# Seven block products for half of the down projection's columns, with the weight differences on GpSimd

## The reference

```python
def swiglu(x, w_gate, w_up, w_down):
    return (jax.nn.silu(x @ w_gate) * (x @ w_up)) @ w_down

h = h + swiglu(rms_norm(h, norm2_g[i]), ffn_w_gate[i], ffn_w_up[i], ffn_w_down[i])
```

## Time and profile before

| what | value |
|---|---|
| median of three runs | 1424.87 us |
| profiled execution, first to last instruction (span) | 1422.4 us |
| TensorE busy | 1395.2 us, 98% |
| VectorE busy | 944.7 us, 66% |
| ScalarE busy | 691.0 us, 49% |
| GpSimd busy | 82.9 us, 6% |
| moved by DMA | 239.47 MB, 168 GB/s on average |
| one ring slot of 1.5 MB, issue to landing (median) | 6.6 us |

### The profile page before, as it was taken

The page is one execution under the profiler, slowest core; times in us unless marked ns, Lnnn a source line. Parts: engine busy times, 40 slices in busy tenths (PEclk is TensorE's granted clock), DMA queues, the critical chain, the costliest instruction groups (busy, mean ns, idle before and its releaser), DMA issues. The chain is left out here.

```text
span 1422.4 us, 25483 instructions
## 1 busy us (share of the span) xinstructions
PE 1395.2 (98%) x10044; PEld 1286.2 (90%) x10044; DVE 944.7 (66%) x1539; ACT 691.0 (49%) x1107; POOL 82.9 (6%) x137
## 2 busy tenths in 40 slices
PE   8999999999999999999999999999999999999997
PEld 8898888999989999899989999999998988899997
DVE  5778567766668666567577666676665676676665
ACT  6764545433454443376654433444433655643342
POOL 1030010000020000000000000100000123000000
PEclk9999999999999999999999999999999999999999
DMA  9344005645526555433356545365554423465540
GB/s 359 135 160 185 2 25 228 222 177 183 197 108 228 209 184 177 178 104 133 120 207 224 189 177 182 129 229 198 194 177 178 149 90 134 177 222 180 194 158 30
DMA packets 33069, 239.47 MB, mean 168 GB/s; under 512 B 6864, under 2 KB 13280, under 8 KB 14304
## 3 DMA queue, kind: packets, MB, share of 16 engines
q1 hardware_dynamic: 30320, 234.84, 45.6%
q10 hardware_dynamic: 2672, 3.58, 0.7%
HBM read 236.15 MB, written 2.25 MB: 168 GB/s over the span
## 5 line engine op out<-in xcount | busy, mean ns | idle before, releaser
L498 PE MATMUL ps<-uT_h,w_gu 128*128 128x256 f32 x3520 | 614.1, 279 | 2.5 <-ACT uT_h L1316 2.5
L498 PEld LDWEIGHTS ps<-uT_h,w_gu 128*128 128x128 f32 x3520 | 538.0, 188 | 13.8 <-issue 5.0
L498 PE MATMUL ps<-uT_l,w_gu 128*128 128x256 f32 x1760 | 478.8, 279 | 0.0
L498 PE MATMUL ps<-w_dn,h_r 128*128 128x512 f32 x1320 | 325.7, 396 | 0.3 <-DVE h_r L2070 0.3
L498 PEld LDWEIGHTS ps<-uT_l,w_gu 128*128 128x128 f32 x1760 | 325.5, 188 | 0.0
L498 PEld LDWEIGHTS ps<-w_dn,h_r 128*128 128x128 f32 x1320 | 239.6, 188 | 51.3 <-issue 1.4
L1368 ACT CAST w_gu<-ring 128x2048 fp32r<-128x2048 f32 x110 | 210.0, 1909 | 156.2 <-PE ps L498 155.6
L2028 DVE TENSOR_TENSOR w_gu<-ring,w_gu 128x2048 fp32r<-128x2048 f32 x110 | 252.1, 2292 | 35.2 <-ACT w_gu L1368 35.2
L2061 DVE TENSOR_TENSOR us<-ps,bc 128x256 f32<-128x256 f32 x110 | 46.5, 423 | 203.2 <-PE ps L498 203.2
L1381 ACT ACTIVATE wk<-wk 128x256 f32<-128x256 f32 x110 | 46.1, 419 | 260.7 <-DVE wk L2059 260.7
L1374 ACT CAST w_dn<-ring 128x1024 fp32r<-128x1024 f32 x110 | 115.7, 1052 | 82.8 <-PE ps L498 82.7
(11 more groups left out here) (398 smaller groups left out, 1696.0 us busy)
## 6 DMA issues: line engine op xcount, KB each, us to landing
ring<-wstream SPq DMA_DIRECT2D x144, 1536.0 KB, 6.6
cst<-consts_in SPq DMA_DIRECT2D x1, 2185.0 KB, 13.7
wk<-t_row ACTq DMA_DIRECT2D x1, 2048.0 KB, 8.0
wk<-masks_in SPq DMA_DIRECT2D x1, 1216.0 KB, 24.1
x<-x_in SPq DMA_DIRECT2D x2, 512.0 KB, 4.7
ring<-wstream SPq DMA_DIRECT2D x1, 1024.0 KB, 8.8
inh<-gains ACTq DMA_DIRECT2D x2, 512.0 KB, 9.6
tri_blocks<-wk SPq DMA_DIRECT2D x3, 256.0 KB, 2.8
```

Source lines behind the costliest of these rows:

```text
L498: return pe.matmul(o, l, r, start=start, stop=stop, skip_group_check=True)
```

## The change

Chunks 0 to 17 are taken in 9 pairs (PAIRS). The columns of the down weights are reordered into four blocks of 256. For two of them, a pair is a product of 2 x 2 blocks: two token tiles by two chunks for h, two chunks by two column blocks for the weights. It is made of seven block products instead of eight, in the form of Strassen and Winograd: four sums of h blocks (forms, on VectorE), four differences of weight blocks (x_diff and y_diffs, on GpSimd), and seven products that are summed over the pairs in seven half banks of PSUM. After the ninth pair VectorE puts them together and adds them to the residual stream (combine). The other two column blocks, and all columns of chunks 18 to 21, are computed as before.

The sums over the pairs need PSUM, so gate and up have one bank each (4 and 6; chunk 1 alone uses 5 and 7). The down part of a chunk comes two steps after its gate and up instead of one: the X products (two of seven, with the even chunk's plain half) after up of an even step, the Y products (five, with the odd chunk's plain half) after up of the next. The factor bc is left out of up and put on the sum of the down products at the end (row_scale). The split of all eight h blocks is one copy on ScalarE and one subtraction on VectorE for each pair. The down weights move in the stream: slot c holds those of chunk c-2, and each feed-forward has one slot more, 23. Six steps are written out before the loop, which has three rounds. Elsewhere some semaphores are merged into one with steps.

```diff
-        LOOPS = (FC - 6) // 4
+        LOOPS = (PLAIN - LOOP_FROM) // 4
+        IN_X = [(0, 0, 7, 256), (2, 768, 5, 0)]
+        IN_Y = [(3, 1024, 0, 0), (5, 1792, 0, 256), (4, 2048, 2, 0), (6, 2304, 5, 256), (7, 2560, 7, 0)]
+        def gu_bank(c, m):
+            return ps[(5, 7)[m] if c == 1 else (4, 6)[m]][:, 0:T]
...
+            def products(p, these):
+                for i, ws, bank, lo in these:
+                    for n, (a, b) in enumerate(PASSES):
+                        last = mm(ps[bank][:, lo:lo + 256], h_r[a][:, i * P:(i + 1) * P], w_d[b][:, ws:ws + 256],
+                                  p == 0 and n == 0 and i in STARTS_BANK, p == PAIRS - 1 and n == 2)
+                return last
...
                 def step(c, r=0):
-                    pe.wait_ge(s["lo_a"], r + (q + c + 1))
-                    if q + c >= 2:
-                        pe.wait_ge(s["h_ready"], r + (q + c - 1))
+                    n, pairs = q + c, 2 * (PAIRS * f + c // 2 - 1)
+                    def up_free():
+                        if c == 1:
+                            spread_rstd(norm)
+                        else:
+                            pe.wait_ge(s["h_mul"], r + (n - (c == 2)))
+                    pe.wait_ge(s["lo_a"], r + (n + 1))
                     if c == 0:
...
                         first_gate_up(norm)
                     else:
-                        gate_up(c, (lambda: spread_rstd(norm)) if c == 1 else None)
-                    if 0 < c < FC - 1:
-                        pe.wait_ge(s["lo_b"], r + (q + c))
-                        pe.wait_ge(s["h_ready"], r + (q + c))
...
-                        down(c - 1, c == 1)
+                        if c > 1:
+                            pe.wait_ge(s["gs_ready"], r + (n - (c == 2)))
+                        gate_up(c, up_free)
...
+                    if 2 <= c < PLAIN + 2:
+                        if c % 2 == 0:
+                            pe.wait_ge(s["bx_ready"], r + (pairs + 2))
+                            pe.wait_ge(s["form_lo"], r + (pairs + 2))
+                            products(c // 2 - 1, IN_X)
+                            for t in range(TT):
+                                last = down_part(c - 2, t, 1)
+                            last.then_inc(s["dx_done"], 2)
+                        else:
+                            pe.wait_ge(s["by_ready"], r + (pairs + 2))
+                            for t in range(TT):
+                                down_part(c - 2, t, 1)
+                            products(c // 2 - 1, IN_Y).then_inc(s["dy_done"], 2)
+                    if PLAIN < c < FC:
+                        if c < FC - 1:
+                            down(f, c - 1)
...
+            def x_blocks(f, p, r=0):
+                i, n = BASE[f"ffn{f}"] + 2 * p + 2, 2 * (PAIRS * f + p)
+                if n:
+                    act.wait_ge(s["dx_done"], r + n)
+                act.copy(w_d[0][:, 0:768], slot(i)[:, 2 * D:2 * D + 768]).then_inc(s["bx_hi"], 1)
+                act.wait_ge(s["bx_diff"], r + (n + 2))
+                act.copy(w_d[0][:, 768:1024], diffs[:, 768:1024]).then_inc(s["bx_hi"], 1)
+            def y_blocks(f, p, r=0):
...
+                act.copy(w_d[0][:, 1024:2048], slot(i)[:, 2 * D:3 * D]).then_inc(s["by_hi"], 1)
+                act.wait_ge(s["by_diff"], r * 2 + (2 * n + 4))
+                act.copy(w_d[0][:, 2048:2816], diffs[:, 2048:2816]).then_inc(s["by_hi"], 1)
+            def forms_hi(f, p, r=0):
...
+                act.wait_ge(s["form_ready"], r * 2 + (2 * n + 4))
+                act.copy(h_r[0][:, :], misc[:, 0:8 * P]).then_inc(s["form_hi"], 2)
...
                     act.activation(sg[:, c % 2, :], sg[:, c % 2, :], ACT.Silu).then_inc(s["silu_ready"], 1)
                     if c + 2 < FC:
                         hi_a(f, c + 2, r, rr)
...
+                    if c < PLAIN:
+                        if c % 2:
+                            forms_hi(f, p, r)
+                        else:
+                            x_blocks(f, p, r)
+                    else:
+                        if c < PLAIN + 2:
+                            hi_b(f, c)
+                        if c == PLAIN + 1:
+                            act.copy(xn[:, 0, 0:512], ps[7][:, :]).then_inc(s["p_copied"], 1)
+                        act.wait_ge(s["h_mul"], n + 1)
+                        hs = c % 2 * 3 * P
+                        act.copy(h_r[0][:, hs:hs + T], sg[:, c % 2, :]).then_inc(s["h_hi"], 1)
...
+            def x_diff(f, p, r=0):
...
+                gp.wait_ge(s["hi_a"], r + (FC * f + 2 * p + 3))
...
+                gp.tensor_tensor(diffs[:, 768:1024], b12, b11, ALU.subtract).then_inc(s["bx_diff"], 2)
+            def y_diffs(f, p, r=0):
...
+                gp.wait_ge(s["hi_a"], r + (FC * f + 2 * p + 4))
...
+                gp.tensor_tensor(t3, b22, b12, ALU.subtract).then_inc(s["by_diff"], 1)
...
+                gp.tensor_tensor(t2, t3, b11, ALU.add).then_inc(s["by_diff"], 1)
...
+                gp.tensor_tensor(t4, b21, t2, ALU.subtract).then_inc(s["by_diff"], 2)
...
                 def step(c, r=0):
...
                     v.wait_ge(s["gu_gate"], r + (n + 1))
-                    v.tensor_tensor(h, ps[4 + c % 2][:, 0:T], bc[:], ALU.mult).then_inc(s["gs_ready"], 1)
+                    v.tensor_tensor(h, gu_bank(c, 0), bc[:], ALU.mult).then_inc(s["gs_ready"], 1)
+                    if c % 2 == 0 and 2 <= c <= PLAIN:
+                        y_lo(f, p - 1, r)
+                    if c % 2 and c < PLAIN:
+                        x_lo(f, p, r)
                     v.wait_ge(s["gu_ps"], r + (n + 1))
-                    v.tensor_tensor(us[:], ps[6 + c % 2][:, 0:T], bc[:], ALU.mult).then_inc(s["us_ready"], 1)
...
+                    v.tensor_tensor(to, two(h), two(up), ALU.mult).then_inc(s["h_mul"], 1)
+                    if c % 2 and c < PLAIN:
+                        forms(f, p, r)
                     if c + 2 < FC:
                         lo_a(f, c + 2, r)
...
+                    elif c % 2:
+                        forms_lo(f, p, r)
+                    if c == PLAIN + 1:
+                        combine(f)
```

More of the change, by code:

```diff
@@ L23 @@
 RING = 4
+PAIRS = 9
+PLAIN = 2 * PAIRS
+LOOP_FROM = 6
 NC_CMP, CMP_STRIDE = 15, 16
@@ L153, in build @@
         w_gu = over("w_gu", [P, 2, 2, 2 * D], "wk")
-        w_dn = over("w_dn", [P, 2, 2, D], "wk", 8 * D)
-        h_r = over("h_r", [P, 2, 2, T], "ffb")
+        w_d = [over(f"w_d{i}", [P, 2816], "wk", 8 * D + i * 2816) for i in range(2)]
+        h_r = [over("h_r0", [P, 8 * P], "ffb"), over("h_r1", [P, 8 * P], "inh", 2 * D)]
         ring_r = over("ring_r", [P, RING, SLOT], "ring")
@@ L549, in _, with gate_up @@
             PASSES = [(0, 0), (1, 0), (0, 1)]
-            def gate_up(j, between=None):
+            def gate_up(j, between):
                 for m in range(2):
-                    if m and between:
+                    if m:
                         between()
@@ new lines, in y_lo @@
+            def y_lo(f, p, r=0):
+                i, n = BASE[f"ffn{f}"] + 2 * p + 2, 2 * (PAIRS * f + p)
+                v.wait_ge(s["by_hi"], r + (n + 1))
+                v.tensor_tensor(w_d[1][:, 1024:2048], slot(i + 1)[:, 2 * D:3 * D], w_d[0][:, 1024:2048].bitcast(F32),
+                                ALU.subtract)
+                v.wait_ge(s["by_hi"], r + (n + 2))
+                v.tensor_tensor(w_d[1][:, 2048:2816], diffs[:, 2048:2816], w_d[0][:, 2048:2816].bitcast(F32),
+                                ALU.subtract).then_inc(s["by_ready"], 2)
+                v.wait_ge(s["by_ready"], r + (n + 2))
+                for k in range(2):
+                    v.sem_inc(s[f"free{(i + k) % RING}"], 1)
@@ new lines, in forms_lo, with lo_b @@
+            def forms_lo(f, p, r=0):
+                n = 2 * (PAIRS * f + p)
+                v.wait_ge(s["form_hi"], r + (n + 2))
+                v.tensor_tensor(h_r[1][:, :], misc[:, 0:8 * P], h_r[0][:, :].bitcast(F32), ALU.subtract
+                                ).then_inc(s["form_lo"], 2)
+            def lo_b(f, c):
+                i, lo = BASE[f"ffn{f}"] + min(c + 2, FC), 2 * D if c + 2 < FC else (c + 2 - FC) * D
+                e, ws = 4 * f + c - PLAIN, c % 2 * D
+                v.wait_ge(s["hi_b"], e + 1)
+                v.tensor_tensor(w_d[1][:, ws:ws + D], slot(i)[:, lo:lo + D], w_d[0][:, ws:ws + D].bitcast(F32),
@@ L2642, in _ @@
               "g23_ready")
-            ffn(0, 1.0)
+            ffn(0, 1.0, rstd(1))
             norm(3)
-            ffn(1, 0.5)
+            ffn(1, 0.5, small[:, 6:8])
             norm(4)
```

344 lines of the change are left out of this document (226 added, 118 removed).

## The result

The changed kernel took **1437.68 us** (median of 4 runs, 1436.37 to 1438.62) where the kernel before, on the same chip, took 1424.99 (1424.51 to 1425.17): a ratio of 1.0089, with a 95% interval of 1.0074 to 1.0103. It is 0.9% slower. The forecast was 1435.5, with 1424 to 1448 around it. The profiled execution spans 1435.9 us, 13.5 more than before; the mean granted clock is 0.994, where it was 0.999.

What follows compares the result with a forecast made beforehand. TensorE, busy 98% of the span, was taken to bound the kernel. -15.75 + 13.6 + 9.25 + 1.45 + 2.1 = +10.65 us on the 1422.4 span, plus 2.5 for launch and end, gave 1435.5 us; range 1424 to 1448.

Steps and rivals of the forecast that it cites:

- gate(2) behind lo_a(2): Step 2 of each feed-forward: TensorE pauses 2.8 us for lo_a(2), 2.4 in feed-forward 0; 13.6 us in all.
- first X products behind form_lo: Pair 0 of each feed-forward: TensorE waits 1.85 us for forms_lo; 9.25 us in five, bounds 6.75 and 17.7.
- gate(3) of feed-forward 1: Feed-forward 1: gate(3) waits for gs(2), which stands behind first_block in VectorE's queue; 1.45 us.
- tails: Ends of feed-forwards 0, 2 and 3: TensorE waits for chunk 21's h, 0.9, 0.9 and about 0.3; 2.1 us.
- The starts: Steps 0 and 1 lose their down part, so TensorE waits twice per start: at gate(2), 13.6 us, and pair 0, 9.25.
- the addition for GpSimd: First pair: 0.5 us, taken once per start, for y_diffs slipping between VectorE's operations; raises the pause from 1.35 to 1.85.
- the prediction's sentence on the rule: First pair: GpSimd and VectorE operations exclude each other; one subtraction let in whole before forms_lo would add 1.2 us.
- The prediction's 2.43 us row: Profile of the kernel before: a GpSimd operation released beside lo_a(1) lasted 2.43 us, ending with it; cited for the exclusion rule.
- The saving: Down products of 9 pairs in 5 feed-forwards: 2.80 us become 2.45 each, 15.75 us less TensorE work.
- The rival of the clock: Clock falls to 1.2 GHz in the starts' pauses, so step 2 runs slower: 1453 to 1467 us; chance 0.05.
- The other steps costed at nothing: Steady pairs without waits, combine's eight additions in step 19, and the 23rd slot's DMA: each costs nothing.
- The faster rival: The starts' pauses do not open, leaving 15.75 less the 2.1 at the end: 1411 us; chance 0.13.

Runs made afterwards that it cites:

- experiment 1: Changed kernel with ScalarE's hi_a(2) ahead of the copy of bc and VectorE's lo_a(2) ahead of the first gate's scaling; 1422.51 us, ratio 0.9988.
- experiment 7: Changed kernel with hi_a(2), lo_a(2) early, first_block spread over steps 2 to 5, last h copy early, and forms_lo(0) ahead of lo_a(3); 1414.81 us, ratio 0.9932.
- experiment 8: Changed kernel with 20 unused 256-column matmuls ahead of the wait for lo_a(2) in each feed-forward; 1437.17 us, ratio 1.0087.
- experiment 2: Changed kernel with feed-forward 1's four first_block operations placed one behind each of steps 2 to 5; 1435.04 us, ratio 1.0074.
- experiment 3: Changed kernel with ScalarE's copy of h for chunk 21 ahead of hi_a of the next feed-forward; 1434.94 us, ratio 1.007.
- experiment 4: Changed kernel without GpSimd's weight differences, ScalarE and VectorE reading the plain weight blocks in the same sizes; 1433.92 us, ratio 1.0061.
- experiment 6: Changed kernel with an eighth product, three more 256-column matmuls, in each pair; 1452.45 us, ratio 1.0194.

## Why the prediction was right

By its own steps, the forecast beside what the profiled execution shows:

| Step | Forecast, us | Measured, us | Shown by |
|---|---|---|---|
| TensorE work taken away, 45 pairs | -15.75 | -13.95 | pair of 16.49 against 16.80 |
| gate(2) behind lo_a(2), five | +13.6 | +12.4 (waits: 13.3) | starts of gate(2), below; experiment 1 |
| first X products behind form_lo, five | +9.25 | +8.4 | 7.24 to 7.33 from gate(2), less 5.6; experiments 7, 8 |
| gate(3) of feed-forward 1 | +1.45 | +2.2 (wait: 2.0) | experiment 2 |
| lower clock behind that wait | 0 | +1.6 | windows; experiment 2 |
| tails | +2.1 | +2.4 (waits: 1.6) | experiment 3 |
| sum | +10.65 | +13.05 | feed-forwards and the gaps behind two of them: +12.9; span: +13.5 |

The measured column goes by the starts of matmuls. The single steps miss by 0.3 to 1.8 us, in both directions; that their sum came within 3 us of the span's change is in part luck.

**The starts** were right in mechanism and size. The chain to lo_a(2) kept its length when the work that covered it was moved to the pairs, and the wait came out within 0.3 us of the forecast. In feed-forward 2 of the kernel before, gate(2) starts 14.82 us after the first gate (TensorE):

```profile
726.64 0.59 PE L498 MATMUL ps<-uT_h,w_gu 128*128 128x256 f32 x3 [0.51 <-ACT uT_h L1316]
...
741.46 0.42 PE L498 MATMUL ps<-uT_h,w_gu 128*128 128x256 f32 x2
```

In the changed kernel it is 14.69 (734.21 to 748.90), although the 2.8 us of down(0) no longer lie between. Over the five starts gate(2) comes 1.6 us sooner than before, and 14.0 us of work come later: 12.4 net. The bare sum of VectorE's list gave 1.35 us for the second pause and the addition for GpSimd made it 1.85; it was 1.67 (8.4 / 5). In the one start of experiment 4 that is free of a fall, the stretch is 0.95 us shorter without GpSimd; the forecast's share for GpSimd was 1.25 (0.75 for x_lo behind b12 - b11, and 0.5 for the y_diffs). The rows of feed-forward 2 divide them, the changed kernel above and experiment 4 below:

```profile
749.10 1.16 DVE L2197 TENSOR_TENSOR w_d<-ring,w_d 128x768 fp32r<-128x768 f32 x1
...
754.23 1.76 DVE L2231 TENSOR_TENSOR h_r<-misc,h_r 128x1024 fp32r<-128x1024 f32 x1
```

```profile
746.27 0.95 DVE L2190 TENSOR_TENSOR w_d<-ring,w_d 128x768 fp32r<-128x768 f32 x1
...
751.06 1.22 DVE L2224 TENSOR_TENSOR h_r<-misc,h_r 128x1024 fp32r<-128x1024 f32 x1
```

forms_lo is 0.54 longer, which the y_diffs' 0.5 met. The 0.75 was too much: x_lo's first piece does not read the difference and began without waiting for it, and it is 0.21 longer. Another 0.13 is lo_a(3), which starts later behind hi_a(3).

**gate(3)** was priced 0.7 us too low. first_block's four operations, taken at 3.12 us, lasted 3.94 beside GpSimd's subtractions, and 3.11 in experiment 4 without them (VectorE, changed kernel and experiment 4):

```profile
440.14 3.94 DVE L2153 SCALAR_TENSOR_TENSOR x<-x,small,inh 128x512 f32<-128x512 f32 x4
```

```profile
439.73 3.11 DVE L2146 SCALAR_TENSOR_TENSOR x<-x,small,inh 128x512 f32<-128x512 f32 x4
```

The Trainium skill (SBUF — State Buffer, "two separate sides") lets such a pair of operations run one at a time, each for a whole instruction. The rows agree in that both lengthen, GpSimd's by 1.95 us on average and VectorE's forms_lo by 0.36. In the first pair, which the prediction's sentence on the rule is about, forms_lo is 0.54 longer, somewhat less than the whole subtraction of 0.73 that it let in. GpSimd's first y_diff, released beside lo_a(3), ends there at 754.91, 0.68 behind the listed start of forms_lo, as if it had slipped in between:

```profile
752.07 2.84 POOL L2025 TENSOR_TENSOR wk<-ring 128x256 f32<-128x256 f32 x1 [2.63 <-ACT w_gu L1434]
```

The prediction's 2.43 us row bears out that the two exclude each other, but not first come, first served: GpSimd's operation is listed as starting at 417.81, ahead of lo_a(1) at 417.92, and yet it is the one that was lengthened, as far as GpSimd's rough listed starts can tell.

**The saving** was 1.8 us too large. The step "7 products x 3 passes = 21 of 256 columns (2.45 us)" priced the pair at 16.45; it is 16.49, and 45 x 0.04 are the 1.8. The down parts of a pair take 2.10 and 3.17 us where the pace of the earlier trace rows gives 2.10 and 3.15, the two gates and ups 11.22 where it gives 11.20. GpSimd isn't the cause, since experiment 4 has the same pair; the cause was not sought further.

**The rival of the clock** was judged on a false ground. "A pause of 2.8 is shorter than the 3.0 of rest after which it was still granted in full" read the earlier trace rows as a bound; the clock did fall, behind 2 of the 5 pauses in the changed kernel (2.1 to 2.8 us), and behind 4 of 5 in experiment 4. Its price was wrong as well, the other way: it added at least half of 5.6 us to each start, but a stretch of 3.4 us at half pace loses 1.6, a start of the changed kernel that waits for form_lo until 7.25 us after gate(2) has slack for that, and experiment 8 shows that it costs nothing there. With form_lo at 6.34, as in experiment 4, it costs the 0.9 between. What did cost was the one fall behind gate(3), 1.6 us, and it was not in the sum. It is a matter of the execution as well: experiment 6 has the same wait and no fall behind it.

**The other steps costed at nothing** held: the pairs have no wait, the additions of combine do not show, and the 23rd slot brings no wait for a transfer.

**The faster rival** was described rightly: without the pauses of the starts it gave 1424.87 - (15.75 - 2.1), 1411. Experiment 7, in which they are all but gone and the tails mended too, gives 1414.8. The pauses were a matter of the order of two lists, ScalarE's and VectorE's, not of the seven products.

Of the 0.6 us by which the stages outside the feed-forwards took longer, one stretch at the lower clock, from 193.2 to 196.6 us and ahead of the first feed-forward, is some 0.4. The rest is open.

## What to carry to other kernels

Work that is taken from the bounding engine, or moved later, may have been the cover of somebody's preparation: before counting the saving, look for what ran behind the removed work and whether its chain got shorter too. Here a saving of 14 us in the pairs was eaten by five starts of some 4.2 us each, and moving a handful of operations in the other engines' lists, ahead of work that nobody waited for yet or behind work that was wanted sooner, gave most of it back (ratio 0.9932). When a fix removes a wait, follow its queue one step further: with forms_lo first, a wait of 0.6 us at gate(3) stands where 1.5 us stood before the X products. And before the difference of two executions is read as the price of an edit, compare them stage by stage: in experiments 3, 4 and 6 a fall of the clock, or the stages around, changed along with it.

## What the runs showed of the hardware that was not expected

- Pauses of 1.98 to 2.8 us, inside feed-forwards in which TensorE otherwise worked nearly all the time, were enough for the granted clock to fall to 0.50 (1.2 GHz), for about 3.4 us, beginning when TensorE was at work again. It was not so each time: behind gate(2), with pauses of 2.1 to 2.8 us, the clock fell in 17 of 25 starts (changed kernel, experiments 2, 3, 4 and 6). In experiment 7, where no wait inside a feed-forward was over 1.06 us, it did not fall in one. The length of the pause doesn't decide alone: ahead of the first feed-forward the clock fell at a wait of 0.78 us in the changed kernel (windows below), and again in experiment 7, but in none of the other kernels, which have the same wait. What else decides is open. The Trainium skill (TensorE: Matmul & The Clock Gate, "What's actually happening") has the gate go back to 1.2 GHz after idling; the runs agree with that, and they show that it can meet a pause of 2 us.

```profile
193.00:194.00 1.00, 0.70 (x4) 0.74 (x5) 0.97 (x2) 0.77 (x1) 0.00 (x0) 0.62 0.00 0
194.00:197.00 3.00, 3.00 (x17) 3.00 (x16) 2.79 (x8) 0.00 (x0) 0.00 (x0) 0.56 0.00 0
```

- A slow stretch need not cost anything: ahead of a wait it takes up time that would have been idle (experiment 8: the same time with and without it).
